# Accumulating DMAs in place of half of the S5 output products, and a later load of the residual's input, in a hybrid SSD / S5 decoder block

## The reference, cut to what matters

```
bu = einsum("gpc,blgc->blgp", b_bar, u)            # complex drive
states = scan(s[t] = lam_bar * s[t-1] + bu[t])     # over the tokens
y = einsum("gcp,blgp->blgc", cmat, states).real + d_skip * u
...
merged = sigmoid(g_a) * y_a + sigmoid(g_b) * y_b
h = h + merged @ w_out
```

## Time and profile before

| | us |
|---|---|
| median of 3 runs | 1687.7 (1687.45 to 1689.55) |
| the profiled execution's own time | 1687.59 |
| its span | 1686.0 |
| PE busy | 1673.8 (99%) |
| DVE busy | 1321.9 (78%) |
| ACT busy | 971.6 (58%) |
| POOL busy | 177.0 (10%) |
| mean granted clock of TensorE | 0.998 of full speed |

### The profile page before, as it was taken

How to read it: one execution, slowest core, us unless ns; L and a number is a source line. 1 busy time by engine, 2 the same in 40 slices (tenths; PEclk the granted TensorE clock), 3 DMA queues, 4 the chain that set the end, 5 groups by cost and what they waited for, 6 DMA issues and landing times.

```text
span 1686.0 us, 24685 instructions
## 1 busy us (share of the span) xinstructions
PE 1673.8 (99%) x8468; PEld 1399.1 (83%) x8468; DVE 1321.9 (78%) x1677; ACT 971.6 (58%) x1271; POOL 177.0 (10%) x262
## 2 busy tenths in 40 slices
PE   9999999999999999999999999999999999999997
PEld 8888888888888888888878888888888888888886
DVE  7999999999998987545765868888888888845555
ACT  7776777667666667434547755444444444454553
POOL 7834201110000000000000200000000000000001
PEclk9999999999999999999999999999999999999999
DMA  7655555554566566666786577777777777756653
GB/s 254 213 185 175 185 173 179 169 181 163 196 218 219 190 220 187 201 197 195 243 266 208 170 231 243 241 241 244 243 243 242 236 245 236 234 190 198 190 188 123
DMA packets 167656, 352.19 MB, mean 209 GB/s; under 512 B 16112, under 2 KB 32672, under 8 KB 167456
## 3 DMA queue, kind: packets, MB, share of 16 engines
q1 hardware_dynamic: 162528, 338.26, 61.9%
q0 software_dynamic: 4336, 12.07, 2.1%
q10 hardware_dynamic: 720, 0.93, 0.2%
HBM read 335.41 MB, written 15.80 MB: 208 GB/s over the span
## 4 chain that ended last, share of the span: by engine, by line
PE 98%; DVE 1%; DMA 1%; SPq 0%; issue 0%; ACT 0%; DVEq 0%; POOL 0%; ACTq 0%; POOLq 0%
PE psum L1792 22%; PE psum L1794 22%; PE psum L1793 22%; PE psum L1753 19%; PE psum L1755 9%; PE psum L1842 1%; PE psum L1878 1%; PE psum L1832 1%; DMA merged_blocks<-flat_m 0%; PE psum L1804 0%; PE psum L1903 0%; PE psum L1879 0%; PE psum L1799 0%; DVE vn L1719 0%; PE psum L1809 0%; DMA quad_m<-merged_blocks 0%
## 5 line engine op out<-in xcount | busy, mean ns | idle before, releaser
L1085 DVE TENSOR_TENSOR wlo<-raw,whi 128x1024 fp32r<-128x1024 f32 x580 | 707.7, 1226 | 319.6 <-ACT whi L646 312.8
L646 ACT ACTIVATE whi<-raw 128x1024 fp32r<-128x1024 f32 x580 | 611.3, 1058 | 576.1 <-PE psum L1794 449.4
L1753 PE MATMUL psum<-act,whi 128*128 128x512 f32 x1088 | 342.6, 396 | 0.0
L1792 PE MATMUL psum<-whi,nw 128*128 128x512 f32 x704 | 274.1, 389 | 0.0
L1794 PE MATMUL psum<-whi,nw 128*128 128x512 f32 x704 | 273.9, 389 | 0.0
L1793 PE MATMUL psum<-wlo,nw 128*128 128x512 f32 x704 | 273.9, 389 | 0.0
L1755 PEld LDWEIGHTS psum<-act,wlo 128*128 128x128 f32 x1088 | 204.4, 188 | 48.3
L1755 PE MATMUL psum<-act,wlo 128*128 128x256 f32 x1088 | 213.8, 278 | 0.0
L1753 PEld LDWEIGHTS psum<-act,whi 128*128 128x128 f32 x1088 | 165.6, 189 | 3.3 <-issue 2.8
L1792 PEld LDWEIGHTS psum<-whi,nw 128*128 128x128 f32 x704 | 132.2, 188 | 27.5
L1794 PEld LDWEIGHTS psum<-whi,nw 128*128 128x128 f32 x704 | 132.2, 188 | 27.3
(11 more groups left out here) (249 smaller groups left out, 2283.9 us busy)
## 6 DMA issues: line engine op xcount, KB each, us to landing
raw<-in_w_up SPq DMA_DIRECT2D x176, 512.0 KB, 4.9
raw<-in_w_zx SPq DMA_DIRECT2D x96, 512.0 KB, 3.5
raw<-in_w_down SPq DMA_DIRECT2D x88, 512.0 KB, 3.8
raw<-in_w_gate SPq DMA_DIRECT2D x64, 512.0 KB, 5.1
raw<-in_w_proj SPq DMA_DIRECT2D x48, 512.0 KB, 4.4
raw<-in_w_bc SPq DMA_DIRECT2D x32, 512.0 KB, 3.5
raw<-in_w_glu SPq DMA_DIRECT2D x32, 512.0 KB, 4.4
raw<-in_w_out SPq DMA_DIRECT2D x32, 512.0 KB, 4.5
```

The source lines that it names most:

```text
L646: fn(whi[:, s, :], raw[:, s, :], ACTF.Copy).then_inc(hi_ready, 1)
L1085: V.tensor_tensor(wlo[:, s, :], raw[:, s, :], whi[:, s, :], ALU.subtract).then_inc(lo_ready, 1)
L1753: mm(psum[:, b + t, :], whi[:, s, cols(t)], x, start=first, stop=False)
L1792: mm(banks[:, t, :], x_hi, high[:, k], start=j == 0 and k == 0, stop=False)
```

## The change

There are two edits.

1. POOL adds, behind each turned-on tile, the rows pairwise inside `st[r]` with two accumulating DMAs: row [1, 1] onto [0, 0] and row [1, 0] onto [0, 1], 128 KB each. TensorE then waits for all eight DMAs of the block (`state_ready`, 16 for each) and multiplies only the two rows of k = 0: 8 matmuls a block in place of 16. For this POOL's queue is ordered anew: the sums of a block stand between the loading of the next input and the filling of `cz`, two foldings move ahead of the rest of the decay rows' series, the loop over blocks 3 to 6 is written out, and the sum of the very last tile stands behind `load_decay(0, 0)`.
2. POOL's load of `h` also waits until the last merged piece has been read back (`m_read` 128).

```
-                pe.wait_ge(x5_ready, blk * 4 + 4)
-                for k in range(4):
+                pe.wait_ge(state_ready, blk * 128 + 128)
+                for k in range(2):
                     for r in range(4):
-                        ins = mm(to[32 * r:32 * r + 32], cz[:, r, (0, 1, 1, 0)[k], :], st[r][:, k // 2, k % 2, :],
-                                 start=k == 0, stop=k == 3)
+                        ins = mm(to[32 * r:32 * r + 32], cz[:, r, k, :], st[r][:, 0, k, :], start=k == 0, stop=k == 1)
...
+            def state_sum(blk, r):
+                pool.wait_ge(x5_ready, blk * 4 + (r + 1))
+                for c in range(2):
+                    pool.dma_start(st[r][:, 0, c, :], st[r][:, 1, 1 - c, :], accum_op=ALU.add).then_inc(state_ready, 16)
+            def state_sums(blk, tiles=range(4)):
+                for r in tiles:
+                    state_sum(blk, r)
...
             horner_steps((11, 9))
+            state_sums(0)
             fill_next(0)
             load_next(1)
             fold(2, 2)
+            state_sums(1)
+            fill_next(1)
+            load_next(2)
+            fold(4, 4)
+            state_sums(2)
+            fill_next(2)
+            load_next(3)
             horner_steps((7, 5, 3))
...
-            fill_next(1)
-            load_next(2)
-            fold(4, 4)
-            fill_next(2)
-            with pool.Fori(3, 7) as i:
-                load_next(i)
-                fill_next(i)
+            state_sums(3)
+            fill_next(3)
+            for blk in range(4, 7):
+                load_next(blk)
+                state_sums(blk)
+                fill_next(blk)
+            state_sums(7, range(3))
             pool.wait_ge(rot_free, 1)
             pool.wait_ge(scr_w, 48)
             load_decay(0, 0)
+            state_sum(7, 3)
             pool.wait_ge(y5_ready, 8)
             load_decay(0, 1)
...
             pool.wait_ge(unit_used, UNIT0["out"])
+            pool.wait_ge(m_read, 128)
             pool.dma_start(h[:, :, :], a["x"]).then_inc(h_in, 16)
```

More of the change, by code:

```diff
@@ L239, in build_program @@
             sem, ("s5_square", "s5_inv", "s5p_ready", "u_ready", "iota_ready", "angm_ready"))
-        ubs_ready, rot_free, bu_used, modulus_ready = map(
-            sem, ("ubs_ready", "rot_free", "bu_used", "modulus_ready"))
+        ubs_ready, rot_free, bu_used, modulus_ready, state_ready = map(
+            sem, ("ubs_ready", "rot_free", "bu_used", "modulus_ready", "state_ready"))
         th_ready, sincos, bu_ready, ang_ready, tab_ready, x5_ready, y5_ready, cz_ready, y5_out, y5_gelu, y5_hi, y5_lo = map(
```

## The result

The changed kernel is slower. Its median is 1694.9 us (1692.6 to 1697.4, 6 runs) against 1687.6 (1687.1 to 1691.2, 6 runs) for the kernel before; the ratio, taken over all runs, is 1.0036, 95% interval 1.0026 to 1.0047. The profiled execution took 1697.4 us with a span of 1695.8; before it was 1687.59 and 1686.0. So the two profiles lie 9.8 us apart, the medians 7.3: the profiled execution is the slowest of its six and has their lowest mean granted clock (0.993; the others have 0.994 to 0.996). The sums over the two spans, here and in the account of the prediction, are of this execution. Two slow executions stand outside everything and are left out of every comparison, one of 9652.8 us of the kernel before and one of 4339.1 us of the kernel with blocks 6 and 7 as before.

The account below looks back on a forecast made before the run. TensorE's own instructions, busy 99% of the span, were taken as the bound. Edit 1 (-4.65 + 0.8 + 2.7 = -1.15) and edit 2 (-1.7) gave -2.85 us on 1687.59: 1684.7, range 1681.8 to 1691.5.

Parts of the forecast that it names:

- the slow rival: In front of the products in every block: a 5.7 us landing makes a 6.45 us chain; 1695.1 us total, chance 0.20.
- The matmuls, 0.93 us a block: TensorE's S5 products: 16 become 8, saving half of 1.86 us a block, 7.4 us over eight.
- "VectorE loses no instruction and gets none", POOL's other work: Around the sums: VectorE's instructions stay unchanged and POOL's other work stays clear of the new chain; no cost.
- Edit 2, - 1.7: Last merged write, without the h load beside it, lands in 3.2 us; TensorE's 1.72 us wait goes, saving 1.7 us.
- The issue, the second one 0.75 us behind the tile: POOL behind each block's last tile: 0.25 us waking, 0.5 to 0.6 an issue, second DMA issued 0.75 us after the tile.
- The landing, 3.4 us for every block: The accumulating DMA of 128 KB lands in 3.4 us, bounds 2.1 and 7.4.
- the chain put at 4.15: From a block's last tile to its products: 0.75 us to the second issue plus 3.4 of landing, 4.15 us.
- the DMA engines are half idle in this stretch: Argument against the slow rival: DMA shares of 0.51 and 0.56 in the stretch of blocks 6 and 7.
- The slack of block 2, "4.0": In blocks 2 to 5 the last tile is ready 4.0 us ahead; a wait of 0.15 at most every other block.
- the 0.8 of the forecast: TensorE's waits for the sums over blocks 0 to 5, together 0.8 us, 0.5 of it in block 0.
- "Blocks 6 and 7 are one term", + 2.7: VectorE has no gap there, so block 7's products start at 449.21 and end at 450.14, not 447.45: +2.7 us.
- the hiding of block 6's wait: Block 6's wait costs nothing extra: its path reaches block 7's products at 447.9, before their start at 449.21.

Follow-up runs that it names:

- the kernel with blocks 6 and 7 as before: The changed kernel without accumulating DMAs in blocks 6 and 7, which keep the 16 products of before; 1684.36 us, ratio 0.9979.
- the kernel with edit 2 alone: The kernel before with only the h loads moved behind the last merged read, no sums; 1685.45 us against 1687.84, ratio 0.9984.
- the profiled run with fillers: The changed kernel with unused matmuls of ones ahead of the products of blocks 6 and 7; median 1693.5 us, ratio 1.0032; the profiled run took 1688.85.

## Why the prediction was wrong

The forecast was 1684.7 with a range to 1691.5. The time, 1694.9, is that of the slow rival (1695.1), but that is luck: the rival has a landing of 5.7 us in every block, 8.9 us of waits in blocks 0 to 5 and no half clock; two of eight landings were nearly that long, the waits made 3.9, and the half clock 6.5.

- *The matmuls, 0.93 us a block.* 0.87 measured in blocks with no wait. Right.
- *"VectorE loses no instruction and gets none", POOL's other work.* Right.
- *Edit 2, - 1.7.* Right in its mechanism, too small by 0.7: it gave 2.4 us, its write landed in 3.2, and the h load cost nothing.
- *The issue, the second one 0.75 us behind the tile.* Right: it begins 0.8 us behind the tile. Its record lasts 1.2 us, where the plain DMA that it was read from lasts 0.59; that is part of the landing, which is counted from the start of the issue.
- *The landing, 3.4 us for every block.* Right for blocks 1 to 6 (3.3 to 3.4; the chain put at 4.15 was 4.2 in block 6), wrong for blocks 0 and 7 (5.1 and 5.4, chains of 6.0 and 6.4). One value was used where every block's wait has its own landing. The argument that "the DMA engines are half idle in this stretch" took a mean: with the sums the mean share is 0.70 from 255 to 302 us where it was 0.54, and in block 6's wait the engines are full (1.03 in the table by stretches).
- *The slack of block 2, "4.0".* It was 2.7 (TensorE was there at 207.69, the tile at 205.00). With 0.87 us gone on TensorE, the tile also came 0.9 us later behind the drive, for which no run has the reason. Blocks 0 to 5 waited 3.9 us for the 0.8 of the forecast: 2.30 by block 0's landing, 1.57 by block 2's slack.
- *"Blocks 6 and 7 are one term", + 2.7: the failing step.* The sum prices a wait at its length and has no term for the clock. It holds that VectorE has no gap to give up, "so the tile of block 7 stays ready at 445.06, counted from the drive of block 6, however fast TensorE is", and that block 6's wait is hidden in block 7's. The drives of block 6, before and after, in TensorE's timelines:

```profile
347.39 1.15 PE L1832 MATMUL psum<-ubs,bz 32*128 32x256 f32 x16
...
348.77 1.15 PE L1853 MATMUL psum<-ubs,bz 32*128 32x256 f32 x16
```

  From there to the end of block 7's products it was 100.1 us (447.45) and became 108.7 (457.46): + 8.7 against the + 2.7 of the sum. The 6.0 us between them have three parts. The tile of block 7 came 100.4 us behind the drive and not 97.7: 2.7. The chain behind it was 6.4 and not 4.15: 2.2. Its products ran at half clock, 1.93 us for 0.93: 1.0. The view of VectorE's waits from 396 to 450, empty in the kernel with edit 2 alone, has in the changed kernel

```profile
DVE wlo L1106 <- ACT whi L667: 2.9, 2, 1.5
```

  which is the first part. In the profiled run with fillers, where the products of block 6 come as late (its chain is 4.4 us) but the clock stays up, the tile of block 7 came 98.2 us behind the drive, 0.5 late. So the hiding of block 6's wait was right to half a microsecond as long as TensorE then ran at 2.4 GHz; most of the 2.7 goes with the half clock behind the wait. That is one run against one, so the split is likely and not settled.
- *The half clock was in no term.* It is 6.5 us of the profiled run. The kernel before has no wait long enough to show it: its one wait of 1.72 us brought none. The Trainium skill (TensorE: Matmul & The Clock Gate, "Part 1: The HAM clock gate") says that the clock falls to 1.2 GHz when TensorE has been idle. These traces agree, with waits of 2.30 us and more; the prediction did not weigh it.

In numbers: + 6.0 in blocks 6 and 7 (8.7 for 2.7), + 1.4 for the half clock behind block 7's products ((4.77 - 1.93)/2), + 1.6 for that of block 0 (3.14/2), + 3.1 for the waits of blocks 0 to 5, + 0.3 for products of 0.87, - 0.7 for edit 2. The - 2.85 of the forecast becomes + 8.9; between the spans it was + 9.8.

## What to carry to other kernels

When TensorE is busy for 99% of the span, a chain through another engine and a DMA that replaces its work must be held against the slack at each place where it is used, not against the mean: here six places had 3.6 to 4.4 us before the change and two had under 1, and those two lost what all eight could gain. A wait of TensorE of 2.3 us and more cost more than its length here, since the clock fell, and every wait hangs on one landing, so price it at the spread of the landings and not at their median. Do the exchange where the slack is, move the reader behind one more unit where it is short, and leave the rest alone: that gave 5.9 us where the change as made lost 7.3.

## What the runs showed of the hardware

- TensorE's granted clock went from 2.4 to 1.2 GHz in or behind each of the twelve waits of 2.30 us and more in these traces (2.30, 2.96, 3.23, 3.36, 3.75, 3.76, 3.90, 4.16, 4.31, 4.67, 5.27 and 7.04 us), and behind none of the ten of 1.21 to 1.72 us. Kernels with accumulating DMAs, with plain copies and with neither agree in that.
- The fall came 1.9 to 5.0 us after the wait had begun, so sometimes only behind the wait, and the half clock stayed for 3.4 us (six times), 6.8 (five times) or 10.2 (behind the 7.04). The longer wait does not always have the longer stretch: 3.4 us belong to a wait of 4.67, 6.8 to one of 3.23.
- Issuing two accumulating DMAs of 128 KB keeps POOL for 1.74 us, two plain ones of the same shape for 1.06. They land in 3.7 and 2.6 us in the median, counted from the start of the issue, and the accumulating ones in up to 8.0 beside the weight loads.
- Small matmuls between two units cost about 0.2 us beside their own time (47.06 us a block for 46.86 with 8 of them, 47.9 for 47.73 with 16), which they don't when they stand behind other small ones.
